# Weighing expert rows with four 64 x 64 products on the quarters of TensorE's array, none on VectorE

## The reference

```python
eidx = jnp.take_along_axis(cidx, sel, axis=-1)      # 8 heads x 16 experts for each token
g = jax.nn.softmax(top_s, axis=-1)
u = pu[eidx]
vv = pv[eidx]
a = jax.nn.gelu(jnp.einsum('thkd,td->thk', u, x).astype(f32))
return jnp.einsum('thk,thkd->td', (g * a).astype(vv.dtype), vv).astype(x.dtype)
```

## Time and profile before

| | |
|---|---|
| median of 3 runs | 1287.94 us (1287.37 to 1290.2) |
| the profiled execution | 1292.07 us, of which the span is 1290.3 us |
| TensorE busy, products / weight loads | 1051.2 us (81%) / 571.2 us (44%) |
| VectorE busy | 850.6 us (66%) |
| ScalarE busy | 398.5 us (31%) |
| GpSimd busy | 420.9 us (33%) |
| transfers | 481.89 MB, 402.68 MB of them gathered rows |
| granted TensorE clock, mean | 0.952 of 2.4 GHz |

### The profile page before, as it was taken

How to read it: one execution, slowest core, us unless ns; L and a number is a source line. 1 busy time by engine, 2 the same in 40 slices (tenths; PEclk the granted TensorE clock), 3 DMA queues, 4 the chain that set the end, 5 groups by cost and what they waited for, 6 DMA issues and landing times.

```text
span 1290.3 us, 11110 instructions
## 1 busy us (share of the span) xinstructions
PE 1051.2 (81%) x3547; PEld 571.2 (44%) x3547; DVE 850.6 (66%) x1983; ACT 398.5 (31%) x1207; POOL 420.9 (33%) x398
## 2 busy tenths in 40 slices
PE   5999685899798999887999777778768777777776
PEld 4796464556455544455555333323323222323222
DVE  3522565898789677787687999984455444444444
ACT  0320241233163443434233333332223222222222
POOL 1000031333232433333234444434334433433331
PEclk9998997999898999998899888989998999999999
DMA  9695099999999999999898899999999999999996
GB/s 373 221 362 220 10 384 383 414 417 359 352 423 402 383 398 422 390 418 400 323 350 328 363 394 395 394 406 410 421 422 378 421 421 421 422 422 421 423 421 251
DMA packets 71723, 481.89 MB, mean 373 GB/s; under 512 B 7680, under 2 KB 16620, under 8 KB 18416
## 3 DMA queue, kind: packets, MB, share of 16 engines
q0 software_dynamic: 55296, 402.68, 77.3%
q1 hardware_dynamic: 15520, 77.72, 15.4%
q10 hardware_dynamic: 848, 0.78, 0.2%
HBM read 475.27 MB, written 5.88 MB: 373 GB/s over the span
## 4 chain that ended last, share of the span: by engine, by line
PE 39%; DMA 28%; DVE 26%; ACT 4%; issue 3%; SPq 0%; POOL 0%; DVEq 0%; ACTq 0%; POOLq 0%
DMA arena<-in_peer_uv,arena 21%; PE ps L1159 18%; DVE arena L1741 11%; PE ps L1170 5%; PE ps L929 4%; PE ps L921 3%; DMA arena<-scratch 3%; DMA arena<-in_w_pq 3%; PE ps L1126 2%; PE ps L1217 2%; DVE arena L1669 1%; DVE arena L1676 1%; ACT arena L715 1%; DVE arena L1670 1%; ACT arena L721 1%
## 5 line engine op out<-in xcount | busy, mean ns | idle before, releaser
L1159 PE MATMUL ps<-arena 128*128 128x512 f32 x1372 | 659.4, 625 | 189.0 <-ACT arena L721 185.5
L574 POOL DMA_INDIRECT arena<-in_peer_uv,arena x384 | 414.8, 1080 | 795.7 <-PE ps L1159 602.1
L1741 DVE CUSTOM_DVE_ANT_0 arena<-arena 128x1024 f32<-128x1024 f32 x380 | 456.6, 1224 | 232.8 <-DMA arena<-in_peer_uv,arena 229.7
L1159 PEld LDWEIGHTS ps<-arena 128*128 128x128 f32 x1372 | 260.0, 198 | 547.1 <-ACT arena L721 276.7
L712 ACT ACTIVATE arena<-arena 128x2 f32<-128x2 f32 (+1 forms) x194 | 39.3, 203 | 586.4 <-DVE arena L1741 580.7
L1170 PE MATMUL ps<-arena 128*128 128x256 f32 x576 | 131.7, 382 | 1.7 <-ACT arena L683 1.7
L1170 PEld LDWEIGHTS ps<-arena 128*128 128x128 f32 x576 | 110.6, 192 | 33.8 <-issue 17.8
L721 ACT ACTIVATE arena<-arena 128x128 f32<-128x128 f32 x343 | 121.4, 395 | 6.4
L601 ACT ACTIVATE arena<-ps 128x256 f32<-128x256 f32 (+2 forms) x79 | 35.7, 468 | 213.8 <-PE ps L1170 77.9
L715 ACT ACTIVATE arena<-arena 128x1 f32<-128x1 f32 x384 | 92.3, 287 | 6.4
L929 PE MATMUL ps<-arena 128*128 128x512 f32 x144 | 67.1, 614 | 0.0
(11 more groups left out here) (229 smaller groups left out, 662.4 us busy)
## 6 DMA issues: line engine op xcount, KB each, us to landing
arena<-in_w_in SPq DMA_DIRECT2D x16, 2048.0 KB, 11.0
arena<-in_w_pq SPq DMA_DIRECT2D x8, 2048.0 KB, 13.2
arena<-in_w_out SPq DMA_DIRECT2D x4, 2048.0 KB, 9.4
arena<-in_peer_uv,arena POOLq DMA_INDIRECT x384
arena<-in_state_C SPq DMA_DIRECT2D x1, 2064.0 KB, 11.9
out_new_C_s<-arena SPq DMA_DIRECT2D x1, 2064.0 KB, 12.2
arena<-in_cache_k SPq DMA_DIRECT2D x4, 512.0 KB, 10.5
arena<-in_cache_v SPq DMA_DIRECT2D x1, 2048.0 KB, 11.2
```

The source lines that it names most:

```text
L574: nc.gpsimd.indirect_dma_start(slots[e % SLOTS], None, d["peer_uv"], bass.IndirectOffsetOnAxis(ap=eidx[:, t, e:e + 1], axis=0)).then_inc(l ...
L1159: last = mm(ps[:, BANKS + half, :], diag[:, k, :], slots[k][:, DM + 512 * half:DM + 512 * half + 512], start=e == 0, stop=e == HK - 1 or ( ...
L1741: last = v.tensor_tensor_reduce(slots[k][:, 0:DM], slots[k][:, 0:DM], hn[t], 1.0, 0.0, ALU.mult, ALU.add, aslot[:, k:k + 1])
```

## The change

All rows are weighed by TensorE: `on_vector` is false for every expert, so `acc` and its add are gone. The weighing of one expert is four products instead of two, each of 64 contracted partitions, 64 output partitions and 512 columns. The diagonal has zeros outside its two 64 x 64 blocks on the diagonal, so token half r (partitions 64 r to 64 r + 63) needs only its own block. Product i takes block r and writes to output half c; r and c both run over 0 and 1. The columns' half is (r + c) mod 2, and the bank is 6 + r. Thus all four quarters of the array (row half r, column half c) are used. In PSUM a bank now holds one half of the tokens: output half r has their first 512 columns, the other output half the last 512. `finish` therefore adds in four pieces of 64 partitions x 512.

```diff
 def on_vector(n, e):
 
-    return n == 0 and (e % 4 == 3 or e % 4 == 1 and 54 <= e < 92)
+    return False
...
                 if n and e == 0:
                     pe.wait_ge(acc_read, n)
-                for half in range(2):
-                    last = mm(ps[:, BANKS + half, :], diag[:, k, :], slots[k][:, DM + 512 * half:DM + 512 * half + 512],
+
+                for i in range(4):
+                    r, c = i % 2, (i + i // 2) % 2
+                    half = (r + c) % 2
+                    last = mm(ps[halves[c], BANKS + r, :], diag[halves[r], k, DA * r:DA * r + DA],
+                              slots[k][halves[r], DM + 512 * half:DM + 512 * half + 512],
                               start=e == 0, stop=e == HK - 1 or (n == 0 and e == HK - 2), skip_group_check=True)
                 last.then_inc(used_p, 1)
...
                 dve.wait_ge(used_p, tensor_count(n, HK - 1))
-                v.tensor_tensor(xr[:, t, 0:512], xr[:, t, 0:512], ps[:, BANKS, :], ALU.add)
-                link(v.tensor_tensor(xr[:, t, 512:1024], xr[:, t, 512:1024], ps[:, BANKS + 1, :], ALU.add))
+                for r in range(2):
+                    tok = slice(64 * r, 64 * r + 64)
+                    for c in range(2):
+                        half = (r + c) % 2
+                        out = xr[tok, t, 512 * half:512 * half + 512]
+                        last = v.tensor_tensor(out, out, ps[64 * c:64 * c + 64, BANKS + r, :], ALU.add)
+                link(last)
                 v.engine_nop().then_inc(acc_read, 1)
-                if n == 0:
-                    link(v.tensor_tensor(xr[:, t, :], xr[:, t, :], acc, ALU.add))
                 link(square_sum(hn[t], xr[:, t, :], 56))
```

## The result

The changed kernel takes 1259.34 us (median of 4 runs, 1259.01 to 1260.51) beside 1287.65 for the kernel before (the three runs shown above and one more): a ratio of 0.9778, 95% interval 0.9761 to 0.9795, or 28.3 us faster. Forecast were 1268.3 us and a sum of -19.6 us. The profiled execution took 1260.51 us, its span is 1258.7. So the change won 9 us more than forecast; the question is where.

A forecast was written before the change was run, and what follows sets the result against it. Bounds by stage: no single engine in the first tile, TensorE at 600 to 707 us, VectorE to 874, transfers in the third tile. -10 - 1 - 10 + 1 + 0.4 = -19.6 us, so 1268.3; range 1250 to 1287, likeliest case 1258 to 1285.

The forecast's parts named there:

- Four abreast, 0.87 us an expert: TensorE's weighing: passes on the four array quarters run together, so an expert takes two waves of 0.43 us, not 1.72 us.
- The rule of the Trainium skill: TensorE's weighing, rival: column quarters sharing rows take turns and wait for weight loads, 2.5 us an expert; 1418 us, chance 0.02.
- A switch of 0.4 us there and back: TensorE: changing between whole-array and quartered products and back costs 0.4 us, bounds 0 and 1, in 64 first-tile units.
- The rival of 1.0 us: TensorE: a switch there and back costs 1.0 us, +7 at 396 to 500 us, about +7 elsewhere; 1297 us, chance 0.06.
- Nine feature units, 11.5 us, taken as 10: Second tile's start, 600 to 707 us: nine units with a feature product each gain 1.28 us on TensorE; 10 us taken.
- First tile -10: First tile, 165 to 600 us: VectorE freed of 51 us, rows dotted sooner, more gathers under way; 10 us, bounds 0 and 27.
- Transfers of 384 GB/s at share 1.01 tell that slower transfers, not slots, cost part of it: First tile, 284 to 396 us: part of the 27 us over the 421 GB/s ceiling comes from slower transfers.
- 707 to 874 us, -1: Second tile: VectorE, busy 156 of 167 us, is the bound and its work doesn't change; gain 1 us, bounds 0 and 12.
- Boundary of second and third tile, +1: Finish before the third tile: two more adds delay the next tile's weighing and the slots behind it; 1 us lost.
- Third tile 0, also at the lower clock: Third tile: transfers alone bound it, so no gain; at TensorE's lower clock an expert takes 1.7 us, as now.
- End +0.4, at the lower clock +1.3: Program's end: last expert falls from 1.98 to 1.1 us, adds cost 1.3 more; +0.4 us, or +1.3 at the lower clock.
- Two abreast, 1336 us: TensorE's weighing, rival: only two quarters run together, 1.72 us an expert, first tile +44; chance 0.05 including one by one.

The follow-up runs named there:

- column halves: All rows on TensorE as whole rows by two column halves of the array, two abreast, against the kernel before: 1331.28 us, ratio 1.0336.
- quartering alone: Quartered products, but VectorE keeps weighing its 41 rows of the first tile, against the kernel before: 1267.64 us, ratio 0.9847; once more 1265.71 us, 0.9845.
- spread routing: Changed kernel with the second tile's seven routings spread over 58 units in place of 42: 1251.0 us, ratio 0.9719 to the kernel before.

## Why the prediction was right, step by step

- *Four abreast, 0.87 us an expert:* right; 1.88 us a pair, the way into the quarters included. The order of the quarters made no difference. The rule of the Trainium skill that was weighed against it (TensorE: Matmul & The Clock Gate, Part 3, on weight loads) would have given 1418 us by the prediction's estimate; the trace does not agree with that rule for column quarters of the same rows, whose sixteen passes end within 1.95 us.
- *A switch of 0.4 us there and back:* right, 0.36. Whole pairs against column halves show the same 0.36. The rival of 1.0 us falls. (Its +7 in the other stages of the first tile did not follow from its own numbers: 10 us of work against 47 free.)
- *Nine feature units, 11.5 us, taken as 10:* mis-sized by the trimming. The units gained 6.88 - 5.53 = 1.35 us each, 12.2 in all, and the stretch 13.0. VectorE's 5.0 us a pair, named as next, did not yet decide.
- *First tile -10:* the size was near, -12.4, but by luck, since its stated reason was mostly wrong. The prediction saw TensorE's time fall by only 13 us, and so put the gain on VectorE's 51. That 13 is a net of two moves which should have been priced one by one: quartering alone takes 87 x 0.85 - 64 x 0.4 = 48 us off TensorE, and is worth 10 to 12 us of the tile (TensorE's busy time fell by 41); handing it 41 experts puts back 41 x 0.87 = 36 (21 to 22 measured), and relieves VectorE of 48 in the same tile: 2 to 3 us of the tile by the stretches. The turn at 396 to 500 us that it feared (29 to 34 us) did no visible harm: the slices there stand at 422 and 423 GB/s.
- *"Transfers of 384 GB/s at share 1.01 tell that slower transfers, not slots, cost part of it":* right, and it splits the tile in two. The first tile in two stages, columns as in the earlier trace rows, before and then after:

```profile
165.00:355.00 190.00, 157.72 (x640) 103.89 (x641) 147.68 (x385) 54.83 (x164) 55.18 (x52) 0.92 1.01 384
355.00:600.00 245.00, 222.16 (x753) 125.05 (x752) 196.52 (x401) 103.85 (x288) 89.38 (x78) 0.97 0.99 404
```

```profile
161.00:346.00 185.00, 140.84 (x876) 87.52 (x880) 129.35 (x371) 58.31 (x176) 55.12 (x51) 0.90 1.01 386
346.00:583.00 237.00, 219.23 (x1185) 108.23 (x1183) 166.78 (x376) 112.52 (x315) 90.09 (x79) 0.96 1.01 422
```

By the ends of the dots, dots 1 to 47 take 171.7 us before, 172.3 after, 170.7 with quartering alone and 171.4 with whole products for all rows: neither half of the change counts there, and the rate stays, although more gathers are under way (4.9 on average instead of 3.9, from the times of issue and landing). All of the gain lies in the other 80 dots, 249.9 us instead of 262.8, at 422 GB/s instead of 404. Of the 27 us over the ceiling 17 lay in the first stage, and 15 of them are still there. Beside its gathers stand some 2,200 packets of 1 KB or less, against 900 behind it; whether these slow it is not tested.
- *707 to 874 us, -1:* right, -0.7, and VectorE the bound, as spread routing shows.
- *Boundary of second and third tile, +1:* wrong, 0: the third tile's first eight dots take 21.0 us before and after, so its two more adds are hidden. Dots 96 to 127, for which the sum had no term, took 2.1 us less. The cause of that is open: column halves, whose pair takes as long as whole products, take 80.3 us there too, and of the kernel before there is one profile.
- *Third tile 0, also at the lower clock:* right; the clock fell to 0.76 and the tile got no longer (its -1.1 is within what profiles of one kernel differ by).
- *End +0.4, at the lower clock +1.3:* the second of the two came, +1.5; the last expert ran at the lower level, 1.98 us and not 1.1. With spread routing it ran at the upper (granted 1.00), and the stretch behind the last dot is 11.4 us instead of 12.3.
- *Two abreast, 1336 us:* its price was near, 1331.28 measured for a kernel that does so (its first tile 34.8 us longer than before, where 44 were reckoned); the changed kernel doesn't.

Of the 8.7 us between -28.3 and -19.6 the stretches account for 2.4 (first tile), 3.0 (second tile's start), 2.1 (dots 96 to 127) and 2.1 (boundary and third tile), less 0.3 (dots 32 to 95) and 1.1 (end): 8.2 us. What is left is far below the scatter of the first stretch.

## What to carry to other kernels

Price the parts of a change one by one before netting them: here one part alone gains 1.5%, the other alone loses 2.1%, and the second gains anything only on top of the first. Where several engines work on the same slots, a busy share does not tell whether they are kept back: in the second stage of the first tile TensorE was busy 91% with transfers at 404 GB/s, and is busy 93% now with 422, beside a VectorE at 70% instead of 80%. An average over a tile can hide a stage that the change does not touch: here its first 48 dots. Splitting the array pays by the waves it saves, and each change between split and whole products has to be counted.

## What the hardware showed unexpectedly

- The granted clock went down where TensorE had less to do: in the third tile from 1.00 (200 of 270 us busy) to 0.76 (148 of 260 us), with pauses for the diagonal before each expert; with whole products there (194 of 260 us busy) it was 1.00 again.
- An add from PSUM of 64 partitions x 512 takes 0.69 us, as long as one of 128 x 512: halving the partitions halves nothing on VectorE.
- Four quarters start 6.6 ns apart, in either order. The Trainium skill (TensorE: Matmul & The Clock Gate, Part 3, Measured speedup vs the span model) gives a span of one product's time plus about 4 ns for each further tile. By it a wave of four would be 0.44 us, an estimate, which these rows can't tell from 0.43 + 3 x 0.0066 = 0.45.
